# Routing stage: the one-hots of the a side made and gated by VectorE in one instruction a token, instead of made by VectorE and scaled by ScalarE

## The reference

```python
qry = (xf @ w_query).reshape(T, PEER_HEADS, 2, PEER_DKEY // 2)
sa = jnp.einsum('thd,nd->thn', qry[:, :, 0], sub_keys_a)
sb = jnp.einsum('thd,nd->thn', qry[:, :, 1], sub_keys_b)
va, ia = lax.top_k(sa, PEER_TOPK)
vb, ib = lax.top_k(sb, PEER_TOPK)
cand = (va[..., :, None] + vb[..., None, :]).reshape(T, PEER_HEADS, PEER_TOPK * PEER_TOPK)
cand_idx = (ia[..., :, None] * PEER_NKEYS + ib[..., None, :]).reshape(T, PEER_HEADS, PEER_TOPK * PEER_TOPK)
top_s, pos = lax.top_k(cand, PEER_TOPK)
experts = jnp.take_along_axis(cand_idx, pos, axis=-1).reshape(T, PEER_HEADS * PEER_TOPK)
gates = jax.nn.softmax(top_s.astype(jnp.float32), axis=-1).reshape(T, PEER_HEADS * PEER_TOPK)
...
act = jax.nn.gelu(jnp.einsum('tkd,td->tk', expert_u[eb], xb), approximate=False)
return jnp.einsum('tk,tkd->td', gb * act, expert_v[eb])
```

## Time and profile before

| what | us |
|---|---|
| median of 3 runs | 4472.89 (4469.64 to 4472.95) |
| the profiled execution's own time | 4512.84 |
| its span | 4511.1 |
| busy in the span: PE | 3705.3 (82%) |
| busy in the span: DVE | 2834.2 (63%) |
| busy in the span: ACT | 908.3 (20%) |
| `hot_a` and `hot_b` on DVE, L2006, 128 instructions | 1870 to 2345 |

### The profile page before, as it was taken

The page is one execution under the profiler, slowest core; times in us unless marked ns, Lnnn a source line. Parts: engine busy times, 40 slices in busy tenths (PEclk is TensorE's granted clock), DMA queues, the critical chain, the costliest instruction groups (busy, mean ns, idle before and its releaser), DMA issues. The chain is left out here.

```text
span 4511.1 us, 40967 instructions
## 1 busy us (share of the span) xinstructions
PE 3705.3 (82%) x13063; PEld 2078.7 (46%) x13063; DVE 2834.2 (63%) x5401; ACT 908.3 (20%) x1899; POOL 1547.3 (34%) x1376
## 2 busy tenths in 40 slices
PE   7899967788835666888849889999899899999995
PEld 1344434455523335777834434444444444444442
DVE  1222334355421213788877889888889898888777
ACT  0111114355401110245541110111111001111110
POOL 1000000000014320000005657666666676667765
PEclk9899976778766778889969989999999999999998
DMA  9211131100034224566529989999999999999997
GB/s 331 84 44 44 45 110 38 47 24 29 25 122 124 87 65 175 186 222 231 199 96 368 334 333 372 376 365 380 374 377 382 365 378 384 383 355 392 389 383 291
DMA packets 372738, 1049.91 MB, mean 233 GB/s; under 512 B 31293, under 2 KB 106109, under 8 KB 367362
## 3 DMA queue, kind: packets, MB, share of 16 engines
q0 software_dynamic: 179728, 649.93, 38.4%
q1 hardware_dynamic: 192818, 397.62, 24.2%
HBM read 979.79 MB, written 67.35 MB: 232 GB/s over the span
## 5 line engine op out<-in xcount | busy, mean ns | idle before, releaser
L2236 PE MATMUL psH<-XT,e_uT 128*128 128x512 f32 x2048 | 970.8, 616 | 67.2 <-ACT e_uT L2273 63.7
L2249 PE MATMUL psY<-e_v,e_W 128*128 128x512 f32 x2048 | 887.1, 595 | 17.5 <-DVE e_W L2315 9.4
L2366 DVE SCALAR_TENSOR_TENSOR acc<-pick_v,pick_w,acc 128x1024 f32<-128x1024 f32 x571 | 733.5, 1285 | 236.3 <-DMA pick_v<-in_expert_v,ids 183.3
L2176 POOL DMA_INDIRECT pick_u<-in_expert_u,ids x576 | 716.9, 1245 | 395.0 <-DVE pick_dot L2350 257.1
L2184 POOL DMA_INDIRECT pick_v<-in_expert_v,ids x576 | 666.1, 1156 | 285.8 <-issue 162.0
L2350 DVE CUSTOM_DVE_ANT_0 e_junk<-pick_u,x_rows 128x1024 bf16<-128x1024 f32 x576 | 702.5, 1220 | 26.9 <-DMA pick_u<-in_expert_u,ids 14.5
L2249 PEld LDWEIGHTS psY<-e_v,e_W 128*128 128x128 f32 x2048 | 390.5, 191 | 511.5 <-issue 498.3
L2236 PEld LDWEIGHTS psH<-XT,e_uT 128*128 128x128 f32 x2048 | 383.9, 198 | 461.4 <-issue 384.9
L400 PE MATMUL ps_p<-w_in_sb,hT 128*128 128x512 f32 x1008 | 440.7, 596 | 0.0
L2273 ACT ACTIVATE e_uT<-psU 128x512 f32<-128x512 f32 x256 | 150.0, 594 | 790.6 <-PE psU L2228 704.0
L400 PEld LDWEIGHTS ps_p<-w_in_sb,hT 128*128 128x128 f32 x1008 | 190.5, 191 | 231.2 <-issue 230.2
(11 more groups left out here) (443 smaller groups left out, 4238.6 us busy)
## 6 DMA issues: line engine op xcount, KB each, us to landing
w_query_sb<-in_w_query SPq DMA_DIRECT2D x36, 2048.0 KB, 8.6
e_u<-in_expert_u SPq DMA_DIRECT2D x128, 512.0 KB
e_v<-in_expert_v SPq DMA_DIRECT2D x128, 512.0 KB
G_d<-G_stage SPq DMA_DIRECT2D x16, 2048.0 KB, 10.8
e_g<-G_d SPq DMA_DIRECT2D x32, 1024.0 KB
w_ada<-in_w_ada SPq DMA_DIRECT2D x12, 2048.0 KB, 8.3
w_in_sb<-in_w_in SPq DMA_DIRECT2D x1, 14368.0 KB, 42.3
pick_u<-in_expert_u,ids POOLq DMA_INDIRECT x576
```

Of the source, the lines that this page charges most:

```text
L2176: pool.indirect_dma_start(gu[:, i % NGU, :], None, io["expert_u"][0], bass.IndirectOffsetOnAxis(ids[:, q % 2, j:j + 1], 0)).then_inc(pu_in ...
L2236: m = pe.matmul(psH[a % 2][:, :], uT[:, a % 2, j, :], XT[:, j, :], start=j == 0, stop=j == KD - 1)
L2249: m = pe.matmul(psY[i % NY][:, :], W[:, (b * NBK + t) % NW, k * P:(k + 1) * P], v[:, t, half_cols(half)], start=t == 0, stop=t == NBK - 1)
L2366: dve.scalar_tensor_tensor(out=sums_q, in0=gv[:, i % NGV, :], scalar=wgt[:, m % 2, o:o + 1], in1=sums_q, op0=ALU.mult, op1=ALU.add).then_i ...
```

## The change

The comparison of `oa` is no longer one DVE instruction of 128x1024 for eight tokens. DVE makes `ob` first, and then issues eight TENSOR_SCALARs of 128x128, one a token, that compare with the pick's number and multiply by its gate, both read from `kT` as [128, 1] operands. The last of them signals `oa_set`. ACT's `gate_a` and the semaphore `oa_hot` are gone. PE's side is as it was.

```diff
-        oa_hot, oa_set, ob_set, g_out, g_kept = sem("oa_hot"), sem("oa_set"), sem("ob_set"), sem("g_out"), sem("g_kept")
+        oa_set, ob_set, g_out, g_kept = sem("oa_set"), sem("ob_set"), sem("g_out"), sem("g_kept")
...
-            def gate_a(i, d, n):
-                act.wait_ge(oa_hot, i + 1)
-                for t in range(GT):
-                    m = act.activation(oa[:, i % NO, t, :], oa[:, i % NO, t, :], ACT.Copy, scale=kT[:, d % 2, 2, n * GT + t:n * GT + t + 1])
-                m.then_inc(oa_set, 1)
-
...
                     if j >= 1:
-                        gate_a((j - 1) * SLOTS + s, j - 1, s)
                         if s >= 1:
                             keep((j - 1) * SLOTS + s - 1)
...
                 if i >= NO:
                     dve.wait_ge(g_out, i - NO + 1)
-                for which, o, done in ((0, oa, oa_hot), (1, ob, ob_set)):
-                    dve.tensor_tensor(o[:, i % NO, :, :], number[:, :].unsqueeze(1).broadcast_to([P, GT, NK]),
-                                      kT[:, d % 2, which, at].unsqueeze(2).broadcast_to([P, GT, NK]), ALU.is_equal).then_inc(done, 1)
+                dve.tensor_tensor(ob[:, i % NO, :, :], number[:, :].unsqueeze(1).broadcast_to([P, GT, NK]),
+                                  kT[:, d % 2, 1, at].unsqueeze(2).broadcast_to([P, GT, NK]), ALU.is_equal).then_inc(ob_set, 1)
+                for t in range(GT):
+                    a, gate = (kT[:, d % 2, which, n * GT + t:n * GT + t + 1] for which in (0, 2))
+                    m = dve.tensor_scalar(oa[:, i % NO, t, :], number[:, :], a, gate, ALU.is_equal, ALU.mult)
+                m.then_inc(oa_set, 1)
```

## The result

The changed kernel takes 4509.55 us (median of 6 runs, 4504.38 to 4512.96); beside it, the kernel before took 4472.7. The ratio is 1.0083, with a 95% interval of 1.0070 to 1.0096: 37 us slower. The forecast was 4496, the direction was right, and the time lies 5.6 us above the range.

A forecast was written before the change was run, and what follows sets the result against it. The prediction took DVE to set the pace, except where four query groups in a row hold PE. Three passes at 16 s - 28.1 plus a last at 16 s - 19.6 gave +23.4 us on 4472.9: 4496, range 4464 to 4504.

The forecast's parts named there:

- The price of the eight: DVE's eight TENSOR_SCALARs per slot: two serial memory scalars, pitch 0.249 us, 1.99 us in all; chance 0.50.
- s: Time of a slot's eight TENSOR_SCALARs on DVE: bounded by 1.56 and 1.99 us, the upper taken.
- 16 s - 28.1: Change in us of each of the first three G-building passes, less DVE's waits: +3.7 at s = 1.99.
- 16 s - 19.6: Change in us of the last G-building pass, with no wait to absorb extra DVE work: +12.2 at s = 1.99.
- the same 1.89 and 0.53: End of a pass: PE's last spread and the step to the next kT keep their old times, in us.
- PE alone sets it in neither case: First three passes: PE does not set their length at s = 1.99 or 1.56; its spreads need 1.89 us each.
- the formula: Sum over all four G-building passes, 64 s - 104 us: +23.4 at s = 1.99, nothing at 1.625.
- The free second scalar: Rival on DVE's eight instructions: second memory scalar costs nothing, pitch 0.195 us, -4 us, total 4469; chance 0.30.
- the free scalars: Rival on DVE's eight instructions: memory scalars cost nothing, s = 1.18, -28 us, total 4445; chance 0.05.
- the slow comparison: Rival on DVE's eight instructions: comparison at 1.04 ns a column plus serial scalars, +58 us, total 4531; chance 0.05.
- The swallowed passes: Rival: DVE's 7 us end-of-pass waits absorb three passes' extra work; only the last grows, +12 us, 4485; chance 0.10.
- ACT's removal: Dropping ACT's eight gatings a slot (2.44 us): worth nothing beyond the pass terms, since ACT waited for DVE anyway.

The follow-up runs named there:

- e8: The changed kernel run once more, unaltered, for a second profile; 4506.3 us.
- e4: The kernel before, with the change made in the last pass alone (slots 48 to 63); 4485.8 us beside 4472.1.
- e1: The changed kernel, its eight TENSOR_SCALARs multiplying by constant 1.0 instead of the gate, so one scalar comes from memory; timing only; 4473.2 us.
- e2: The changed kernel, its eight TENSOR_SCALARs comparing with and multiplying by constants, so no scalar comes from memory; timing only; 4451.7 us.
- e5: The changed kernel with 12 extra identity transposes on PE in slots 0, 1 and 9 of the first three passes and every last-pass slot; 4508.8 us.
- e11: The kernel before, with the change made in the first three passes only; 4492.1 us beside 4473.9.
- e3: The kernel before, with DVE comparing the a side in eight one-scalar TENSOR_SCALARs ahead of hot_b, ACT still scaling by the gates; 4480.7 us.

## Why the forecast was right in sign and 14 us short

- **The price of the eight.** The choice was right: the second scalar costs as much as the first. Its size was off: 60 ns and not 54, s = 2.05 and not 1.99. That is 64 x 0.06 = 3.8 us. The 54 were a difference of durations between unlike instructions in other places (227 and 281 ns); the same instruction with and without the scalar has 220 and 280.
- **The first three passes.** 16 s - 28.1 is +4.7 us at s = 2.05; measured +5.6, +4.3 and +9.9 (in e8 +5.2, +4.3, +6.5). The working spread the old waits evenly; by pass they are 11.8, 12.0 and 10.3 us, so the third had less to take from, which fits its growing most even in e8. The waits went as the working had it: that for `rstd` and the buffer are gone, that for `kT` is 1.66 us in three of the six ends of passes in the two profiles, and 1.6 was expected.
- **The last pass.** 16 s - 19.6 is +13.2 at s = 2.05; measured +14.65 in the changed kernel, +14.6 in e8, +13.05 in e4. Its chain up to the last hot_b is 13.3 us longer (13.65 expected); the rest is the last spread of 3.78 us.
- **The term that is missing.** The prediction let every matmul take its old time: "the same 1.89 and 0.53", and held that "PE alone sets it in neither case". This step failed. In the changed kernel's profile PE ran the last spreads of the first and last pass in 3.0 and 3.8 us and a query group of the third in 13.75, at the lower clock. Its price can be read where DVE or the last store waits for PE: the wait for `kT` is 1.3 us above the 1.66 in the first pass and 3.4 above it in the third, and from the start of the last spread to the last store it is 4.87 us, not 3.14. That is 6.4 us, and 2.7 in e8, where the third pass has none of it. What the formula leaves is 34.5 - 27.2 = 7.3 us and 3.4. The prediction had put this term at nothing, and the 4 us left above were for gaps of issue. Why the clock falls there in one execution and not in the other stays open.
- **The sum.** 23.4 predicted, 3.8 for the price and 2.7 to 6.4 for the clock give 30 to 34; measured are 31 and 34.5 in the stage and 36 and 37 in the whole. The 2 to 5 us outside the stage are not explained. In the five profiles without any gating by ACT (changed, e1, e2, e5, e8) the first `kT` comes at 1825.4 to 1830.1 us, 1827.3 in the mean, and in the seven that keep it wholly or in part (that of before left out) at 1818.5 to 1827.7, 1823.1 in the mean; that may be chance.
- **The rivals.** The free second scalar, the free scalars and the slow comparison fell with the three durations. The swallowed passes fell with e11. ACT's removal was said to be worth nothing beyond the terms of the chain; that those terms are large, 13 us in the stage, is what e3 beside e1 shows (7.5 in the medians).
- **The range.** Its upper end was the forecast plus 8 us. The sum is 512 times one unmeasured pitch, so 10 ns of error in that are 5 us, and nothing was left for PE. The 7 ns more in the pitch and PE's 6.4 us give 4506, past the end.

## What to carry to other kernels

When one wide instruction is split into small ones to fold in a second operation, count the fixed part of each and, by itself, every [128, 1] scalar read from memory. Here the fixed parts were paid for by the faster columns, and the scalars were all of DVE's extra time. Multiply the pitch, not the duration, and ask which engine's time ends the stage. Work that is taken off an engine pays only in the slots where that engine was the last to come, so put the fused form there alone. Where a wait of TensorE gets longer, look at what it does next: those matmuls may run at the lower clock.

## What was not expected of the hardware

The second scalar from memory is as dear as the first, 60 ns in the duration and in the pitch (220, 280, 341 ns at 128x128 float32). And TensorE can stay at the lower clock for the whole of a 14 us stretch in which it never stops (granted clock 0.50, 64 matmuls in 13.75 us), while in another execution of the same program the same 64, after waits about as long, take 7.26 us.
